# A cache ring of four buffers in place of six, and a residual stream that stays on chip

## What is computed

```
for layer in range(2):
    hp, hs = rmsnorm(yp, g[0]), rmsnorm(ys, g[0])
    if layer % 2 == 0:   # differential attention and gated linear attention (GLA) behind one projection
        mp = even_mixer(hp, ...)                 # prompt: causal attention over its own 512 tokens
        k_past = cache_k[li, page_table]         # samples: attention over 4096 cached tokens each,
        v_past = cache_v[li, page_table]         # 4 heads x 128 values a token, rows picked by a page table
        ms = even_mixer(hs, ..., attend to k_past, v_past)
    else:
        mp, ms = odd_mixer(...)                  # conv, RG-LRU, gelu gate
    yp, ys = yp + rmsnorm(mp, g[1]), ys + rmsnorm(ms, g[1])
    yp = yp + rmsnorm(sq_relu_mlp(rmsnorm(yp, g[2]), w_up, w_down), g[3])   # the same for ys
```

## Time and profile before

| | |
|---|---|
| median of 3 runs | 1546.75 us (1538.38 to 1546.87) |
| the profiled execution | span 1541.8 us; its own run time is not listed beside it |
| input projection | 30 to 190 us of the span |
| prompt units | 222 to 366 us |
| GLA units and the last V loads | 366 to 530 us |
| output projection, MLPs, odd layer | 530 to 1542 us |
| read from memory, written to it | 239.99 MB, 7.73 MB |

### The profile page before, as it was taken

One profiled execution on the slowest core, in us unless ns is written; L12 is line 12 of the kernel. 1 busy time (PEld: TensorE's weight loads), 2 busy tenths in 40 slices (PEclk: granted clock), 3 DMA queues, 4 the chain that ended last, 5 costly groups with the idle time before them and its releaser, 6 DMA issues.

```text
span 1541.8 us, 26106 instructions
## 1 busy us (share of the span) xinstructions
PE 1406.3 (91%) x11324; PEld 1266.3 (82%) x11324; DVE 882.3 (57%) x1156; ACT 516.7 (34%) x839; POOL 328.7 (21%) x264
## 2 busy tenths in 40 slices
PE   4999957788778698999999999899989999999997
PEld 3999933345334398999999999899989999999997
DVE  3398978766988526624435343689556344353443
ACT  3323254433423424312212122469443122131233
POOL 1085768865777100000000000000000000000000
PEclk8999979877676799999999999999999999999999
DMA  9477699988989831232322322222212323223211
GB/s 320 137 264 232 236 327 382 369 324 326 346 322 346 300 109 55 86 106 83 97 97 82 99 94 83 83 83 83 85 55 88 105 83 101 92 83 103 90 55 56
DMA packets 126856, 249.32 MB, mean 162 GB/s; under 512 B 5251, under 2 KB 107415, under 8 KB 110096
## 3 DMA queue, kind: packets, MB, share of 16 engines
q0 software_dynamic: 18432, 134.23, 22.9%
q1 hardware_dynamic: 103616, 107.13, 21.5%
q10 hardware_dynamic: 4696, 6.32, 1.3%
HBM read 239.99 MB, written 7.73 MB: 161 GB/s over the span
## 4 chain that ended last, share of the span: by engine, by line
PE 58%; issue 25%; DVE 7%; POOL 4%; DMA 3%; ACT 3%; ACTq 0%; POOLq 0%; DVEq 0%
PE PS L1881 46%; PE PS L2074 2%; POOL PROD L680 2%; DMA KV<-in_cache_v,CIDX 2%; DVE SC L1352 1%; PE PS L2216 1%; POOL KV L747 1%; DVE ST L1584 1%; PE PS L2061 1%; PE PS L2158 1%; DMA XSIN<-in_x_sample 1%; PE PS L1865 1%; PE PS L2179 1%; PE PS L2116 1%; PE PS L1975 1%
## 5 line engine op out<-in xcount | busy, mean ns | idle before, releaser
L1881 PE MATMUL PS<-H_hi,W_hi 128*128 128x260 f32 x1936 | 397.7, 287 | 16.7 <-DVE H_lo L1327 9.7
L1881 PE MATMUL PS<-H_hi,W_lo 128*128 128x260 f32 x1936 | 393.4, 285 | 0.0
L1881 PE MATMUL PS<-H_lo,W_hi 128*128 128x260 f32 x1936 | 393.0, 285 | 0.0
L1881 PEld LDWEIGHTS PS<-H_hi,W_hi 128*128 128x128 f32 x1936 | 303.2, 191 | 22.3 <-issue 17.7
L1881 PEld LDWEIGHTS PS<-H_hi,W_lo 128*128 128x128 f32 x1936 | 301.9, 191 | 0.0
L1881 PEld LDWEIGHTS PS<-H_lo,W_hi 128*128 128x128 f32 x1936 | 301.7, 191 | 0.0
L1285 DVE TENSOR_TENSOR W_lo<-RAW,W_hi 128x2048 fp32r<-128x2048 f32 x90 | 208.2, 2313 | 125.9 <-ACT W_hi L810 125.8
L810 ACT ACTIVATE W_hi<-RAW 128x2048 fp32r<-128x2048 f32 x90 | 171.8, 1909 | 266.1 <-PE PS L1881 265.5
L1881 PE MATMUL PS<-U_hi,W_lo 128*128 128x260 f32 x1024 | 206.4, 283 | 0.0
L1881 PE MATMUL PS<-U_lo,W_hi 128*128 128x260 f32 x1024 | 206.0, 283 | 0.0
L1881 PE MATMUL PS<-U_hi,W_hi 128*128 128x260 f32 x1024 | 206.0, 282 | 0.0
(11 more groups left out here) (304 smaller groups left out, 1433.8 us busy)
## 6 DMA issues: line engine op xcount, KB each, us to landing
RAW<-in_w_up SPq DMA_DIRECT2D x32, 1024.0 KB
RAW<-in_w_down SPq DMA_DIRECT2D x32, 1024.0 KB
RAW<-in_w_in_even SPq DMA_DIRECT2D x13, 1024.0 KB
RAW<-in_w_in_odd SPq DMA_DIRECT2D x8, 1024.0 KB
RAW<-in_w_out_even SPq DMA_DIRECT2D x4, 1024.0 KB
RAW<-in_w_out_odd SPq DMA_DIRECT2D x4, 1024.0 KB
x_saved<-X ACTq DMA_DIRECT2D x1, 2080.0 KB, 9.3
X<-x_saved SPq DMA_DIRECT2D x1, 2080.0 KB, 7.8
```

The source lines that it names most:

```text
L1881: t = MM_(PS[:, 2 * bank + j, 0:HALF], w[:, ch.slot, k, cols], x[:, k, half], start=k == 0 and n == 0, stop=k == KT - 1 and n == 2)
```

## The change

`X` keeps its region to itself. The two ring buffers in it, its write to memory, its read back and the waits for both are gone. The ring has four buffers, and since `RING` is taken from the list's length, POOL's loop now issues load i behind the release of load i - 4. All else is as it was.

```diff
     KV4 = sb("KV4", [P, 4, 4, 512], F32, r_kv)
-    KV2 = sb("KV2", [P, 2, 4, 512], F32, r_x)
-    KV = [KV4[:, i] for i in range(4)] + [KV2[:, i] for i in range(2)]
+    KV = [KV4[:, i] for i in range(4)]
     RING = len(KV)
...
-    xsave = nc.dram_tensor("x_saved", [P, KT * T], F32, kind="Internal").ap()
...
-                sp.wait_ge(v_used, 62)
-                sp.dma_start(X[:].rearrange("p k t -> p (k t)"), xsave).then_inc(x_saved, 16)
             load(Chunk(C_OUT0 + j), stage_dram(a["w_out_even"][0], 0, slice(256 * j, 256 * j + 256)))
...
-            if i == 4:
-                po.wait_ge(x_saved, 16)
-                po.wait_ge(hf_ready, KT)
             if i < LOADS:
                 kind, n = ORDER[i]
                 po.indirect_dma_start(KV[i % RING].rearrange("p n f -> p (n f)"), None, cache[kind],
...
         squares(0, X, x_first_ready)
-        act.dma_start(xsave, X[:].rearrange("p k t -> p (k t)")).then_inc(x_saved, 16)
         scaled_hi()
...
         copies(C_OUT0, 0)
-        ve.wait_ge(x_saved, 32)
         opening(C_MLP0, 1, 0, 8, 2, 16)
```

More of the change, by code:

```diff
@@ L311, in trunk @@
     v_sent = sem("v_sent")
-    x_saved = sem("x_saved")
     dg_ready = sem("dg_ready")
```

## The result

The changed kernel takes 1614.59 us (median of four runs, 1611.84 to 1620.35) where the kernel before, on the same chip, takes 1546.64. The ratio is 1.0453, with a 95% interval from 1.0425 to 1.048: slower by 68 us. The forecast was 1594 (1567 to 1622); half of its chance lay on 1580 to 1609, and the time came out above that.

A forecast was written before the change was run, and what follows sets the result against it. PE bounds the input stage; from 222 to 530 us the nearly full DMA engines bring in the cache. Saved X 0, prompt units 17, GLA units 27 and last loads 3 give +47 on 1546.75: 1594 us, range 1567 to 1622.

The forecast's parts named there:

- The saved X: Dropping X's write and read back, with the fifth and sixth K loads issued later in the input stage: 0 us.
- Prompt units: Prompt stage: V1's load is issued later and lands late, +17 us over 15 periods (0 to +30).
- The loop: Prompt units: V1's matmuls to next product 8.2, to V1's issue 3.8, landing 7.7; 19.7 us per two units, 9.85 each.
- K loop: Prompt units: product, issue, landing of K, next product; 8.0 to 10.2 us, said to bind no harder.
- GLA units: GLA stage: V2 is issued behind K1's product and delays the clamp in six units, +27 us (19 to 42).
- +3.1 and +5.9: Clamp delays from late V2 read in two GLA units, the one around 440 us and the next; mean 4.5 us.
- lateness adds up: Rival, 0.20: V1 and V2 of GLA units both wait, loads queue up, PE's clock falls further; +70 us, 1617.
- Last loads and seventh unit: End of the cache: later issue of the last eight V loads, plus the seventh GLA unit; +3 us (0 to 6).
- Short landings: Rival, 0.22: with at most three loads under way each lands in near 5.5 to 5.7 us; about +25, 1572.
- The 27 us that I gave for that estimate: The forecast's sum if a 1 MiB load took the skill's fitted 4.4 us: about 27 us rather than 47.
- Not slower: Rival, 0.07: DMA throughput alone sets the pace, so the ring's depth costs nothing; 1547 us.
- What would show it: Expected profile signs: prompt products near 9.9 us apart, V waits three or four times 13.6 us, about 300 GB/s.

The follow-up runs named there:

- e1: The kernel before with four ring buffers instead of six, X still saved and read back: 1612.08 us, ratio 1.0435.
- e7: The kernel before (six buffers, X saved) with the loads of the prompt units alone issued two entries later: +2.20%.
- e8: The kernel before (six buffers, X saved) with the loads of the GLA units and the last V loads alone issued two entries later: +2.34%.
- e9: The changed kernel with six extra zero-weight matmuls on PE before V2 in six GLA units: time the same within its interval.
- e4: The kernel before (six buffers) with each K product in its own place in POOL's list, not one entry ahead: +0.53%.
- e6: The changed kernel (four buffers) with a GLA unit's loads in the order K V K V V K instead of K V K V K V: 16 us gained.

## Why the prediction came out as it did

**The saved X, 0.** Right: e1 (1.0435) and the changed kernel (1.0453) have overlapping intervals, and POOL's last product ahead of the prompt units starts at 219.41, where it was 219.50. That POOL issues its fifth and sixth K loads behind two products costs nothing there.

**Prompt units, +17 (0 to +30), measured +27 (+23 in e1).** The loop was the right one, and e7 shows that lateness in this stage alone costs 34 us (with units of 11.09). Its landing was right: 7.7 assumed; 7.8, 7.5 and 6.8 us on the chain. Two pieces were too small. From V1's matmuls to the next product I took one reading of before, 8.2 us; now it is 9.4 (303.14 to 312.50) and 10.4 (324.68 to 335.11). In the unit that I read, V1's matmuls took 1.07 us; those on the new chain, behind waits of 4.7 and 6.0 us, take 1.94 (those between them, at 313.31 and 334.20, still 1.07 and 1.06). That reading belonged to a clock that the change itself takes away from this loop. From the product to V1's issue I took 3.8, from the median issue of 1.0 us; the chain has 3.8 once and 4.6 twice (an issue of 1.8 us). Had I used the 4.6 that I had read and the 1.94 of the second V1 in the earlier trace rows, the loop would have been 8.2 + 0.9 + 4.6 + 7.7 = 21.4, the unit 10.7 and the term 26. That the K loop "binds no harder" didn't follow from its own numbers (10.2 at a landing of 7.7 is more than 9.85), but it held: POOL's products waited 8 times, 12.9 us, for a K load, and the prompt periods that end in such a wait are the shorter ones, 8.7 to 9.7.

**GLA units, +27 (19 to 42), measured +38** (10.6 up to the first clamp, of which some 4 belong to the prompt loop, since e8, with prompt units as before, has 6.9 there; and 27.4 for the five periods after it). The step is right in each part: V2 issued 2.5 us behind K1's product, landing in 5.8 to 6.1, and the clamp behind it. What failed is the mean of +3.1 and +5.9. The +3.1 supposed that V2 to clamp takes 3.5 us where the clock is up, and that DVE's hold on the clamp absorbs a part. Once V2 is late in every unit, PE sits idle before it in every unit, and the piece is 5.9 in each (5.9, 5.8, 5.9 and 5.9 in the four units from 469 on). e9 shows the two values of the piece beside each other, the one behind 0.6 and the other behind 5.2 us of idle time. With +5.9 in six units the term is 35, against 38 - 4 = 34. V1 of the GLA units, which the forecast had late only in its far end, is waited for too (16.7 us), but the five periods grew by 27.4 and 5 x 5.9 is already 29.5: these waits add nothing that can be seen. So this part of "lateness adds up" was true, with its clock of 0.64; the other part was not, V2's landing never reached 7, nothing queued up ahead of it.

**Last loads and seventh unit, +3 (0 to 6), measured +3.5.** Close in this execution, and in part by luck: e8, e9 and e1 have +6.1, +8.5 and +9.7 in the same stretch. The term is too small.

**The rivals.** Short landings: true of the GLA units, not of the prompt units, and not in its time. All cache landings of e8 from 366 to 530 us, where its loads are held, against 5.6/7.7/9.9 in the earlier trace rows:

```profile
DMA to landing us min/median/max: 5.5/5.9/6.9
```

But with 5.7 us the forecast had already put V2's landing there. In the prompt units the median falls only from 8.6 to 7.6 (before and e9, 222 to 366 us), and V1's landings on the chain of the changed kernel are 6.8 to 7.8, so 1572 was not reached. The 4.4 us that follow, as an estimate, from the fit of the Trainium skill (DMA: Bandwidth & Descriptors, section on the anatomy of one DMA) were reached by none of the landings on the chain, 5.5 us at the least. The 27 us that I gave for that estimate don't follow either: put in place of 5.7 and 7.7 in the sum, 4.4 gives 22. Lateness adds up, 1617: nearest in size, and right in its clock. Not slower: no. What would show it held, except for sizes: the products came 10.7 us apart and not 9.9, PE's waits grew sixfold and not three- to fourfold (59.8 of the 81.3 us in V1 of the prompt units and V2 of the GLA units), and GB/s fell to 296 and 277, a little under 300.

So the mechanism stands by e7, e8 and e1. The sum was 21 us short, in the prompt and the GLA term alike: two pieces were read at a clock which the change lowers, and one issue was taken as 1.0 us where the chain has 1.8 twice. The range held because it was wide enough for that.

## What to carry to other kernels

Write the new loop out as a closed chain, and take each of its pieces as it is where the engines already wait, not as it is in the mean or where they are busy: in the changed kernel the V loads' matmuls behind waits of 3.0 to 7.6 us all ran at the lower clock, and took nearly twice the time (1.93 against 1.06 us). In a ring of buffers count the entries by which each load goes out later, and find the long operation that stands on the issuing queue between; moving that operation by one entry was worth nearly half of two buffers here, and with all six buffers it cost 0.5%. Don't count the waits as time: e4 takes 12 of 13.6 us of PE's waits away and isn't faster. The first buffer taken away was cheap here and the second was not: 20 us, then 49.

## What the hardware showed that I had not expected

- TensorE after 5.2 us without work ran its next matmuls at half rate (1.93 against 1.06 us), and stayed there for all of the 5.9 us up to the clamp; after 0.6 us it ran at full rate (e9). The wait alone doesn't decide it: in the changed kernel the same matmuls took 1.93 us after 0.57 us without work (451.69) and 1.94 after none (476.42).
- The issue of an indirect DMA of 1 MiB holds POOL for 0.93 to 1.06 us mostly (from 222 us on in the changed kernel), but for 1.8 to 2.0 us in several places behind a product (315.02, 324.11 and 337.62 us in the changed kernel), and then lies on the path.
- A load of 1 MiB from issue to landing, on the changed kernel's chain: 5.5 to 6.1 us with none issued right ahead of it, 6.8 to 8.1 where another was; in e6 8.6 and 9.1 behind two (457.37, 479.62). At a DMA share of 0.90 a load alone took 5.7, at 0.76 5.5 to 6.1.
